# Differential attention scores as two fp32r products of stacked high and low parts, and gate rows spread in one fp32r pass

## The reference

```python
bias = where(dist >= 0, -slopes * dist, -inf)             # dist = t - s, slope 1/4, 1/16, 1/64, 1/256 by head
scores = einsum('bhcqd,bhcsd->bhcqs', q_blk, kh) * 64 ** -0.5 + bias      # c = 0, 1
p = softmax(scores);  p = p[:, :, 0] - lam * p[:, :, 1]
out = einsum('bhqs,bhse->bhqe', p, vh)
...
lfc = log_sigmoid(fg)                                     # forget gates, 4 heads
b = cumsum(lfc);  logD = b[j] - b[s] + i[s], masked to s <= j
m_row = max over s;  Dm = exp(logD - m_row)
Sm = (q k^T) * Dm;  h = (Sm v) / max(|row sum of Sm|, exp(-m_row))
```

## Time and profile before

| | |
|---|---|
| runs of the kernel | 2433.56 us median of three (2433.08 to 2436.03) |
| profiled execution | 2433.92 us |
| its span, first to last instruction | 2432.1 us |
| TensorE busy, granted clock | 2306.5 us, 0.985 of full speed |
| VectorE, ScalarE, GpSimd busy | 1157.1, 703.9, 1023.7 us |
| attention stage of block 2 | from 1424 to about 1753 us of the span |
| mLSTM stage | from there to about 2100 us |

### The profile page before, as it was taken

One profiled execution on the slowest core, in us unless ns is written; L12 is line 12 of the kernel. 1 busy time (PEld: TensorE's weight loads), 2 busy tenths in 40 slices (PEclk: granted clock), 3 DMA queues, 4 the chain that ended last, 5 costly groups with the idle time before them and its releaser, 6 DMA issues.

```text
span 2432.1 us, 27427 instructions
## 1 busy us (share of the span) xinstructions
PE 2306.5 (95%) x9910; PEld 1752.2 (72%) x9910; DVE 1157.1 (48%) x1205; ACT 703.9 (29%) x1108; POOL 1023.7 (42%) x821
## 2 busy tenths in 40 slices
PE   6999998899899999999999879999999999999998
PEld 5777755487688888888886656666666775788877
DVE  5864355446643333434327884555364444611123
ACT  4243355532311111111112333333434324200112
POOL 3533400186544444444446542212244542444475
PEclk8999999999999999999999999999999999999999
DMA  4111100122111111111112310000101110111143
GB/s 189 53 35 35 35 9 9 78 87 78 61 48 47 52 43 52 44 50 51 44 52 72 121 44 27 26 26 19 33 27 35 43 34 26 44 44 52 51 149 120
DMA packets 33635, 130.56 MB, mean 54 GB/s; under 512 B 3736, under 2 KB 4120, under 8 KB 32800
## 3 DMA queue, kind: packets, MB, share of 16 engines
q1 hardware_dynamic: 30960, 111.39, 14.2%
q10 hardware_dynamic: 2608, 18.25, 2.0%
HBM read 117.04 MB, written 12.58 MB: 53 GB/s over the span
## 4 chain that ended last, share of the span: by engine, by line
PE 82%; DVE 9%; ACT 5%; issue 3%; DMA 1%; POOL 1%; SPq 0%; DVEq 0%; ACTq 0%; POOLq 0%
PE PG L645 13%; PE PG L651 13%; PE PG L650 13%; PE PG L1172 5%; PE PG L1178 5%; PE PG L1177 5%; PE PG L992 2%; PE PG L1218 2%; PE PO L1019 1%; PE PO L1241 1%; PE PT L1006 1%; PE PO L1315 1%; PE PG L698 1%; PE PG L704 1%; PE PG L703 1%
## 5 line engine op out<-in xcount | busy, mean ns | idle before, releaser
L540 POOL TENSOR_TENSOR WH<-WR,zero 128x512 fp32r<-128x512 f32 x380 | 420.7, 1107 | 1297.2 <-PE PG L645 678.6
L543 POOL TENSOR_TENSOR WL<-WR,WH 128x512 fp32r<-128x512 f32 x380 | 539.0, 1418 | 29.8
L645 PE MATMUL PG<-HH,WH 128*128 128x512 f32 x1136 | 449.2, 395 | 2.5 <-issue 1.4
L651 PE MATMUL PG<-HH,WL 128*128 128x512 f32 x1136 | 442.9, 390 | 0.0
L650 PE MATMUL PG<-HL,WH 128*128 128x512 f32 x1136 | 442.8, 390 | 0.0
L645 PEld LDWEIGHTS PG<-HH,WH 128*128 128x128 f32 x1136 | 213.7, 188 | 53.0 <-issue 6.1
L650 PEld LDWEIGHTS PG<-HL,WH 128*128 128x128 f32 x1136 | 213.6, 188 | 46.0 <-issue 2.2
L651 PEld LDWEIGHTS PG<-HH,WL 128*128 128x128 f32 x1136 | 213.7, 188 | 44.9
L1172 PE MATMUL PG<-HH,WH 128*128 128x512 f32 x544 | 231.2, 425 | 5.4 <-ACTq L1975 2.8
L1178 PE MATMUL PG<-HH,WL 128*128 128x512 f32 x544 | 214.2, 394 | 0.0
L1177 PE MATMUL PG<-HL,WH 128*128 128x512 f32 x544 | 213.4, 392 | 0.0
(11 more groups left out here) (504 smaller groups left out, 4088.7 us busy)
## 6 DMA issues: line engine op xcount, KB each, us to landing
WR<-weights SPq DMA_DIRECT2D x196, 512.0 KB, 3.5
RAW<-x SPq DMA_DIRECT2D x8, 512.0 KB, 8.2
x_spill<-X ACTq DMA_DIRECT2D x1, 4096.0 KB, 12.8
X<-x_spill ACTq DMA_DIRECT2D x1, 4096.0 KB, 12.2
x_spill<-X ACTq DMA_DIRECT2D x4, 1024.0 KB, 5.3
X<-x_spill ACTq DMA_DIRECT2D x8, 512.0 KB, 3.8
y<-RAW SPq DMA_DIRECT2D x7, 512.0 KB, 5.0
POSI<-positions ACTq DMA_DIRECT2D x1, 512.0 KB, 15.0
```

What stands on the lines that cost most here:

```text
L540: pool.tensor_tensor(WH[:, slot, part], WR[:, slot, part], zero[:, :].to_broadcast([P, HALF]), ALU.add).then_inc(w_hi, 1)
L543: pool.tensor_tensor(WL[:, slot, part], WR[:, slot, part], WH[:, slot, part].bitcast(F32), ALU.subtract).then_inc(w_split, 1)
L645: m = pe.matmul(out[:, cut], WH[:, slot, w], hi[:, cut], start=n == 0, stop=False)
L651: m = pe.matmul(out[:, cut], WL[:, slot, w], hi[:, cut], start=False, stop=last)
```

## The change

Scores: the operands of each map are 64 dimensions on 128 partitions, of which the other 64 were zero but for two positional rows. Now the other 64 hold a second part. `QHL` has the high queries on one half and the low ones on the other, `KHH` the high keys on both; `QHA` has the high queries and the positional rows, `KLA` the low keys and the scaled positional rows. The sum of `QHL` by `KHH` and `QHA` by `KLA` gives all but low by low. Both are fp32r.

Forget gates: the weights and biases of the gates are repeated, so that eight rows hold each gate twice. Four of them go by DMA to `[128, 32]`, log-sigmoid is made there, and two DMAs bring them back into rows 0 to 3 and 4 to 7. `GR` holds high parts in rows 0 to 3 of its groups and low parts in rows 4 to 7, as fp32r; the selector adds both, so a single fp32r product spreads a row exactly. The sums, scans and part of the rows' splitting stand at other places of VectorE's program. The turned values of head 0 go through `PO` and are copied after the first tile. In the mLSTM, both rows are spread as 1024 columns of `PT`: row 0 at the end of a head, row 1 after the first score block of the next.

```diff
@@ TensorE @@
-            g.before(pe, 3)
-            turn(g.psum(3), DVT0[:, :]).then_inc(g_ready, 1)
+            turn(POf, DVT0[:, :]).then_inc(v_turned, 1)
...
-                        pe.matmul(out[:, h * HALF:end], DQ[:, c, t * P:(t + 1) * P],
-                                  DK[:, c, h * HALF:end], start=True, stop=end != (t + 1) * P)
+                        rows, keys = slice(t * P, (t + 1) * P), slice(h * HALF, end)
+                        pe.matmul(out[:, keys], QHL[:, c, rows], KHH[:, c, keys], start=True, stop=False)
+                        pe.matmul(out[:, keys], QHA[:, c, rows], KLA[:, c, keys], start=False,
+                                  stop=end != (t + 1) * P)
...
             spread(hb, 6, selM[:, 0, :], GR)
-            spread(hb, 8, selM[:, 1, :], GR)
...
+                def spread_wide(n):
+
+                    for h in range(2):
+                        m = pe.matmul(PT[:, h, :], selM[:, n, :], GR[:, halves(h)], start=True, stop=True)
+                    m.then_inc(m_wide, 1)
...
+                    if j == 0:
+                        pe.wait_ge(m_mn, 2 * i + 2)
+                        spread_wide(1)
                     if j == 1:
+                        pe.wait_ge(m_me, i + 1)
                         pe.wait_ge(m_vop, i + 1)
...
+                    pe.wait_ge(m_sel, i + 2)
+                    pe.wait_ge(m_abs, i + 1)
+                    spread_wide(0)
                     pe.wait_ge(m_v, i + 2)
                     unit("mlstm", 9, i, ML_UNITS, 1)
                     turn_halves(hb, 8, MVT, (w_used[1], w_used[0]))
-                    pe.wait_ge(m_sel, i + 2)
-                    spread(hb, 10, selM[:, 0, :], GR)
-                    spread(hb, 12, selM[:, 1, :], GR)
                     next_head(20, 24)
@@ ScalarE @@
+            flat = [FLAT[:, n, :] for n in range(5)]
+            act.dma_start(flat[0], GROWS[0][0:4, :]).then_inc(forget_flat, 16)
...
-            log1p_rows(1, GROWS, 2)
+            log1p_rows(1, flat, 2)
...
-                act.dma_start(DQ[rows, c, :], aug_in[0]).then_inc(aug_loaded, 16)
-                act.dma_start(DK[rows, c, :], aug_in[1]).then_inc(aug_loaded, 16)
+                for n in range(2):
+                    act.dma_start(DP[rows, 1, n, :], aug_in[n]).then_inc(aug_loaded, 16)
+            act.wait_ge(forget_made, 1)
+            for at in (0, 4):
+                act.dma_start(GROWS[2][at:at + 4, :], flat[0]).then_inc(forget_back, 16)
...
-            for buf, src, scale, done in ((DQ, NQ, 0.125, d_q), (DK, NK, 1.0, d_k)):
-                act.activation(buf[0:64, 0, :], src[0:64, :], ACT.Copy, scale=scale)
-                act.activation(buf[64:128, 1, :], src[64:128, :], ACT.Copy, scale=scale).then_inc(done, 1)
+            def keys_high():
+
+                act.activation(KHH[0:64, 0, :], NK[0:64, :], ACT.Copy)
+                act.activation(KHH[64:128, 1, :], NK[64:128, :], ACT.Copy).then_inc(d_khi, 1)
+                act.activation(KHH[64:128, 0, :], NK[0:64, :], ACT.Copy)
+                act.activation(KHH[0:64, 1, :], NK[64:128, :], ACT.Copy)
+
+            def queries_high(out, done):
+
+                act.activation(out[0:64, 0, :], NQ[0:64, :], ACT.Copy, scale=0.125)
+                act.activation(out[64:128, 1, :], NQ[64:128, :], ACT.Copy, scale=0.125).then_inc(done, 1)
+
+            act.wait_ge(aug_k, 1)
+            queries_high(QHL, d_qhi)
+            keys_high()
+            queries_high(QHA, d_qb)
...
                     act.wait_ge(d_scores, i * (2 * TT) + 2 * TT)
-                    act.activation(DK[0:64, 0, :], NK[0:64, :], ACT.Copy)
-                    act.activation(DK[64:128, 1, :], NK[64:128, :], ACT.Copy).then_inc(d_k, 1)
+                    keys_high()
                 next_half(6)
+                if not last:
+                    hb.wait_free(act, 0)
+                    hb.wait_free(act, 1)
+                    queries_high(QHL, d_qhi)
                 transposed(TT - 1)
+                if not last:
+                    queries_high(QHA, d_qb)
                 next_half(7)
...
+                    if j == 1:
+                        act.wait_ge(m_den, i)
+                        act.wait_ge(m_wide, 2 * i + 1)
+                        act.activation(ME[:, :], PTf, ACT.Exp).then_inc(m_me, 1)
...
                     next_half(7)
+                    act.wait_ge(m_wide, 2 * i + 2)
+                    act.activation(MN[:, :], PTf, ACT.Copy).then_inc(m_mn, 2)
                     for m in (8, 9):
...
-                if not last:
-                    gate_rows_spread(hb, 10, i + 1, i + 1)
@@ VectorE @@
+            def high_and_low(rows, high, out):
+
+                step(dve.tensor_copy(high, rows))
+                return dve.scalar_tensor_tensor(out, high.bitcast(F32), v("low_rows")[0:8], rows,
+                                                ALU.mult, ALU.add)
...
+            dve.wait_ge(forget_flat, 16)
+            flat = [FLAT[:, n, :] for n in range(5)]
+            step(dve.tensor_scalar(flat[0], flat[0], -1.0, None, ALU.mult))
+            softplus(flat, None, None, 3)
+            dve.tensor_scalar(flat[0], flat[0], -1.0, None, ALU.mult).then_inc(forget_made, 1)
...
+            def keys_low(head):
+
+                dve.wait_ge(d_khi, head + 1)
+                for rows, c in ((slice(0, 64), 0), (slice(64, 128), 1)):
+                    ins = dve.tensor_tensor(KLA[rows, c, :], NK[rows, :], KHH[rows, c, :].bitcast(F32), ALU.subtract)
+                ins.then_inc(d_k, 1)
...
-            step(dve.tensor_scalar(GROWS[0], GROWS[0], -1.0, None, ALU.mult))
-            softplus(GROWS, None, None, 3)
...
             dve.wait_ge(aug_loaded, 64)
-            slopes()
+            for rows, c in ((slice(64, 66), 0), (slice(0, 2), 1)):
+                step(dve.tensor_copy(QHA[rows, c, :], DP[rows, 1, 0, :]))
+                step(dve.tensor_scalar(KLA[rows, c, :], DP[rows, 1, 1, :], 0.25, None, ALU.mult))
             dve.sem_inc(aug_set, 1)
+            queries_low(0)
+            keys_low(0)
...
+            gate_sums()
+            gate_scan()
+            gate_inputs()
+            ROTATED = 3
+            DiffHead(0).tile(0)
+            dve.wait_ge(v_turned, 1)
+            dve.tensor_copy(DV[:, :, :], POf.rearrange("p (t n) -> p t n", t=TT)).then_inc(d_vop, 1)
             select(0)
-            ROTATED = 3
-            gate_sums()
-            DiffHead(0).tile(0)
-            gate_scan()
             DiffHead(0).tile(1)
-            gate_maxima()
+            gate_maximum(4, 0)
             DiffHead(0).tile(2)
+            gate_maximum(3, 32).then_inc(gate_rows, 1)
```

More of the change, by code:

```diff
@@ L194, in program @@
         DPT = at("DPT", 188, [P, TT, HALF])
[L196 to L197 removed]
+        GR = at("GR", 156, [P, S], F32R)
+        GROWS = [RAW[0:8, n, :] for n in range(4)] + [RS[0:8, :], DO[0:8, :]]
+        GHIGH = RAW[0:8, 1, :].bitcast(F32R)
+        FLAT = at("FLAT", 172, [P, 6, 32])
         ACOL = at("ACOL", 24, [P, TT, ML_HEADS])
[L199 removed]
+        selM = at("selM", 25, [P, 2, P], F32R)
         MQ = at("MQ", 0, [P, S])
@@ L1964, in convolved @@
                     act.activation(buf[:, :], MC[n][:, :], ACT.Silu).then_inc(m_q, 1)
-            def gate_rows_spread(hb, m0, head, read=None):
-                for n, (buf, fn, done) in enumerate(((MN, ACT.Copy, m_mn), (ME, ACT.Exp, m_me))):
-                    if n == 1 and read is not None:
-                        act.wait_ge(m_den, read)
-                    for m in (m0 + 2 * n, m0 + 2 * n + 1):
-                        hb.ready(act, m)
-                        act.activation(buf[:, halves(m)], hb.bank(m), fn).then_inc(done, 1)
-                        act.wait_ge(done, 2 * head + (m % 2 + 1))
-                        act.sem_inc(hb.free(m), 1)
             for n in range(2):
@@ L1991, in _ @@
             convolved(0)
-            gate_rows_spread(hb, 6, 0)
+            for m in (6, 7):
+                hb.ready(act, m)
+                act.activation(MN[:, halves(m)], hb.bank(m), ACT.Copy).then_inc(m_mn, 1)
+                act.wait_ge(m_mn, m - 5)
+                act.sem_inc(hb.free(m), 1)
             def mlstm_head(i, last=False):
@@ new lines, in queries_low @@
+            def queries_low(head):
+                dve.wait_ge(d_qhi, head + 1)
+                for rows, other, c in ((slice(0, 64), slice(64, 128), 0), (slice(64, 128), slice(0, 64), 1)):
+                    ins = dve.scalar_tensor_tensor(QHL[other, c, :], NQ[rows, :], 0.125,
+                                                   QHL[rows, c, :].bitcast(F32), ALU.mult, ALU.subtract)
+                ins.then_inc(d_q, 1)
+            g.wait_free(dve, 0)
+            step(dve.memset(GROWS[1], 1.0))
@@ L2749, in _ @@
             dve.wait_ge(aug_loaded, 64)
-            slopes()
+            for rows, c in ((slice(64, 66), 0), (slice(0, 2), 1)):
+                step(dve.tensor_copy(QHA[rows, c, :], DP[rows, 1, 0, :]))
```

(18 more changed lines are left out.)

115 lines of the change are left out of this document (61 added, 54 removed).

## The result

The changed kernel takes **2400.05 us** (median of four, 2399.06 to 2403.09); the kernel before, on the same chip, 2433.48 (median of four). The ratio is 0.9863, 95% interval 0.9845 to 0.9880: 33.4 us faster. The prediction was 2401, its range 2394 to 2411.

The account below looks back on a forecast made before the run. TensorE, busy 95% of the span and 82% of the chain, was taken to bound the kernel. Terms 20.0 + 1.2 - 3.0 + 2.3 + 10.6 + 1.7 = 32.8 us off 2433.6 gave 2401 us, range 2394 to 2411.

Parts of the forecast that it names:

- Score products: Attention scores: four fp32r products replace two fp32 ones; 5.0 us a head in tiles 4 to 7, 1.2 over heads 1 to 3.
- The margin of 0.2 us: Tiles 4 to 7: the exponential ends at 1481.14, the second map starts at 1481.37; this gap was to stay.
- rival (b): Attention heads: score saving half eaten by a late second maximum or negative margin, some 2 us a head, 2409; chance 0.09.
- End of a head: Three attention head ends: ScalarE's added casts delay the last half fill's evacuation and the value product; minus 3.0 us.
- Way into the stage: Before the first attention scores: narrow log-sigmoid starts scores near 1416 instead of 1424; 2.3 us kept after moved gate work.
- rival (a): Log-sigmoid at the attention start: every flat operation waits a GpSimd split, fifteen take 18 us instead of 8, 2411; chance 0.13.
- the 1408: Sign of error at the attention start: the prediction is wrong if the flat log-sigmoid rows come after 1408.
- mLSTM boundaries: Between mLSTM heads, three times: wide fp32r spreads let fills go on 3.55 us earlier; 10.6 us, between 6 and 12.
- Before mLSTM head 0: Ahead of the first decay: ScalarE no longer exponentiates the second row there; 1.7 us saved.

## Why the prediction was right, point by point

**Score products: right, a little low.** I had 5.0 us a head for tiles 4 to 7 and 1.2 for tiles 1 to 3 of three heads, 21.2 in all; putting the old price back costs 22.7, 5.3 to 6.0 a head. The parts are sized a little differently. In tiles 4 to 7 the eight maps with their masks take 6.9 us a head where they took 11.4, 4.5 and not 5.0: I had set 1.75 for two products with the mask against 0.94 for four without it, and it is 1.05 with it. The transposes and value products between them give another 0.3. So tiles 4 to 7 have some 19.4 of the 22.7, and tiles 0 to 3 the other 3.3, where I had 1.2 for heads 1 to 3. The margin of 0.2 us that rival (b) rested on never turned: the unused half of the products still bought 12.1 us. Rival (b) is out.

**End of a head: right.** 1.0 us a boundary by the moved casts, 3.0 for three, predicted 3.0. As predicted it is the bank of the last half fill: TensorE's wait for it is 4.0 us in all and was 1.1.

**Way into the stage: the gain was right (2.3 at tile 1's scores, 2.3 at its transposes), the path to it was not.** The step that failed is that about half of the fifteen flat operations would be held up by a split and the rows be ready near 1404. The flat rows were ready at 1407.7 in the zero of before, the scores began at 1421.6 and not 1416. They took 11.8 us, where I had 8 and rival (a) 18: two operations wait for each pair of splits and one or two slip in between, and so ten of the fifteen were held up, not half. With GpSimd still, five of them took 1.1 us, so it is the splits and nothing of their own. ScalarE's casts stood behind that result, which I had in the account, and the 1408 beyond which I had called myself wrong was nearly reached. One more step was put at nothing. I had the evacuation of the values at 1415 and the scores near 1416; behind that evacuation TensorE must still turn the values, 1.97 us (1.04 in the earlier trace rows), and after 0.90 more the scores start.

The Trainium skill (SBUF — State Buffer, "SBUF: two separate sides") says that a VectorE operation with two SBUF inputs, or in a two-port mode, and a GpSimd operation shut each other out for a whole instruction. The traces agree in kind: 0.18 to 0.19 without splits, up to 1.31 beside them, also for operations with one input (0.95 and 1.31 above). What they don't bear out is the price that rival (a) had made of it, a whole split for each of fifteen.

The gain held because two errors met, and that is luck. VectorE ended the low operations at 1418.3 in that zero, not 1415.6, and the gate work then took the 9.5 us that I had put down: tile 1's scores came at 1428.8, 2.5 late. But from there to the turn of tile 1 I had 3 us more than before for the copy of the turned values, the selectors and the maxima, and it is 10.4 us as before. I had added the copy and the selectors there and not taken off the scan of 2.90, which had left; the maximum of tile 1 comes 1.03 us after its scores start and came 2.31 after. VectorE then waits 1.12 us for TensorE's fill.

**mLSTM boundaries: right.** Predicted 3.55 a boundary; the second scores of successive heads are 79.8, 79.8 and 79.5 us apart, before 83.6, 83.6 and 85.0: 3.8, 3.9 and 5.5. The last holds about 1.5 of clock (the kernel before ran at 0.83 from 1945 to 1955; the changed one had 1.00 from 1920 to 1999). The mechanism is the predicted one: from the `MSUM` product at the head's end to the first fill it is 5.97 us (1814.90 to 1820.87) where it was 9.84 (1834.91 to 1844.75), 3.9 less, and the fill waits 0.75 for ScalarE's copy. Full fp32 spreads give back 1.2 of them each.

**Before mLSTM head 0: wrong, 0.3 instead of 1.7.** The step that failed read the 1.7 us between the exponents (1776.1) and the decay (1777.82) as the exponential of the second row. The exponential ended by 1776.2. What lay between was a wait of 0.33 and a table load of 1.28, and the load stays: 1756.49 above. The exponents end at 1756.38 now, 1.40 ahead of the decay instead of 1.71.

**The sum.** 20.0 + 1.2 - 3.0 + 2.3 + 10.6 + 1.7 = 32.8 predicted, 33.4 measured. By the trace the parts are: 2.3 for the start, 20.0 for the heads with their ends (18.2 predicted), 0.3, 13.1 for the mLSTM (10.6 predicted) with some 1.5 of clock, and 2.3 lost behind it to the clock. That the total is off by 0.6 only is luck: the errors offset each other.

## What to carry to other kernels

Before a chain on VectorE is made short by making its operations small, look at what GpSimd does beside it: 15 operations cost 11.8 us next to back-to-back splits, and twelve of the same cost 0.22 each where GpSimd had a pause. Lay small chains into such pauses. Price work taken off a helper engine by the waits that TensorE can still lose (3.7 us), not by the work (8.5). And where moved work stands in a queue behind a wait, the first fix may show nothing until the second one is made: 0.1 us alone, part of 13 together.

## What was not expected of the hardware

- A GpSimd split costs a VectorE operation about the same whether it has 32 or 1024 columns: 128 x 32 takes 0.18 without one and up to 1.31 beside one, a positional row of 2 x 1024 takes 0.68 and up to 1.67.
- Kernels with the same code up to there reach the same instruction at places up to 6 us apart (1375.30 to 1381.60), with the granted clock of an unchanged stretch at 0.99 and 0.96. A difference of 1 to 2 us in a median of five says little here. Distances within one trace repeat within 0.1 where the clock does not fall (tiles 4 to 7 of a head: 29.4 to 29.5 us), and less well where it does (from the first mask to tile 4 of heads 1 and 2: 21.0 to 22.2).
- An idle TensorE costs twice. After the waits at the start a fill took 4.1 to 4.8 us from first to last product instead of 2.6 (at 1.2 GHz for the most part, not 2.4), and where an earlier start cut the wait in two, two fills did.
